# Projection chunks issued in halves instead of quarters on TensorE, in a decoder step with forgetting attention and gated linear attention

## The chip, the cores and the metric

The kernel runs on one core of a Trainium2 chip. The metric is the device time of one execution in microseconds (us); lower is better. A change of about 0.5% is the least that a measurement of this kernel can tell from none.

## The reference, cut to what matters

One layer of a decoder for a prompt of 1024 tokens and for 8 sequences with 8 new tokens each (64 columns more). Both are normalised and multiplied by one weight matrix, and two branches use the parts of the result:

```python
h = _rmsnorm(x, ln_g)
z = h @ w_in
fq, fk, fv, ff, fg, gq, gk, gv, glr, gg, ma, mb = jnp.split(z, SPLIT_POINTS, axis=-1)
...
o_f = _fox_prompt(fq, fk, fv, logf)      # softmax attention with a forget bias, 8 heads of 64
o_f = _fox_sample(..., cache_k, cache_v, cache_logf, page_table)   # 8 x 32 pages of 128 keys
o_g, s_end = _gla(gq, gk, gv, la, s0)    # 4 heads, state 128x256, chunks of 64 tokens
...
m = jax.nn.sigmoid(ma) * a + jax.nn.sigmoid(mb) * b
return x + m @ w_out
```

Everything is float32. The product `h @ w_in` is the largest piece of work: the kernel calls it the projection.

## The kernel before, in words

**Projection.** The weight matrix comes as tiles of 1024 x 128. For each tile n the 1088 token columns are done in three chunks c of 384, 384 and 320 columns. One chunk is 8 steps of contraction (KT_ = 8), and each step is three matmuls, since float32 is split into a high and a low part: `w_hi` with `h_hi`, `w_hi` with `h_lo`, `w_lo` with `h_hi` (L284, in `WeightStream.project`). So a chunk is 24 matmuls into one PSUM bank, and its last one raises the semaphore `w_projected`. Two banks take turns (`ring`), so the first matmul of a chunk waits on `z_read` until the chunk two before has been read out, and on `w_lo_set` for the tile's weights.

**Two stages that interleave.** The projection is independent work with which TensorE fills the time in which other work waits for ScalarE (ACT) or VectorE (DVE). The order is written out by planners ahead of time as one list of steps, and every engine walks the same list in its own order, waiting on semaphores only. A projection chunk stands in that list as four steps `("z", n, c, part)`, part 0 to 3, a quarter (6 matmuls) each. Between them the planners put the other steps, by estimated costs.

- `fox_order` (stage 1, forgetting attention of the prompt, `build_fox`): for head pair i and tile t of 128 queries: scores `sc` (L1061, TensorE), `sm` (L940 and L945, DVE: mask, bias, row extreme), `ex` (L803, ACT: exp), `pt` (L1071, TensorE: transposes of the probabilities into a bank of the lift ring, copied out by DVE at L566 for the first head and by ACT at L722 for the second), `pv` (L1084, L1089: weighting of the values), and `vt`, `kt`, `nm` (L1035, L1051).
- `schedule` (stage 2, `build_gla`): decode attention over pages (`kt`: four transposes of one page of keys, L1891, copied out by ACT at L1510 or DVE at L1391 in turn; `sc` L1906; `pt` L1922; `pv` L1939; `pn`, `pnv`, `od`) and gated linear attention (`att` L2005; `u` L2012, whose result DVE adds to the state at L1831; `o` L2019 and L2022; `og` L2030; `satt`, `so`, `sstate`; `decay`, `vturn`, `kturn`).

**The lift ring.** All transposes of pages and probabilities go through two PSUM banks that take turns: before the lifted step k, TensorE waits for the copy of step k-2. This wait is in `wait_bank`.

Stage 1 ends near 460 us of the trace, stage 2 near 1330 us. Behind them, four tiles of gates and `build_merge` project whole chunks; they don't use the part numbers.

ACT and DVE handlers stand on some `z` steps too (the split of the next weight tile into `w_hi` and `w_lo`, L254 and L259, at part 1 of a chunk), and SP issues the load of the next tile at part 1 of chunk 1.

Of the kernel before, what the change touches and what calls it, by code (L numbers as in the profile page):

```python
# [30 lines left out]
KT_ = D // P  # L31
# [259 lines left out]
FOX_PARTS = 4  # L291
# [145 lines left out]
def build_fox(nc, ins, outs, scratch, gates, sem, sb, psum, bank, con, vec, cc, vv, epsb, gq8, stream, os_fm, q_s, k_s, newb, glr):  # L437


    with ExitStack() as ctx:  # L440
# [128 lines left out]
        with nc.Block() as block:  # L569
# [422 lines left out]
            def _(pe):  # L992
# [32 lines left out]
                def z(n, c, part):  # L1025
                    if n < 2 and part == 0:
                        pe.wait_ge(h_lo_set, 2 * (3 * c + 3))
                    stream.project(pe, n, c, range(part * KT_ // FOX_PARTS, (part + 1) * KT_ // FOX_PARTS))

                def turn(st, src, p):  # L1030
                    wait_bank(pe, *st)
# [60 lines left out]
                def page_suffix(g):  # L1092
# [5 lines left out]
                              start=True, stop=True).then_inc(lifted, 1)  # L1098

                run(pe, {"xt": turn_x, "ff": forget, "lt": turn_logf, "z": z, "vt": v_turn, "kt": k_turn, "nm": norm_sum, "sc": scores, "pt": turn_prob, "pv": weigh, "lf": page_suffix})  # L1100


PARTS = 4
# [147 lines left out]
def build_gla(block, ins, outs, scratch, gates, sem, sb, psum, bank, cc, vv, epsb, stream, os_fm, q_s, k_s, newb, glr):  # L1251
# [7 lines left out]
    with ExitStack() as ctx:  # L1259
# [89 lines left out]
        for st in steps:  # L1349
            if st[0] in LIFTED:  # L1350
                n = len(lift_of)
# [530 lines left out]
        def _(pe):  # L1882
# [110 lines left out]
                turn(i, kdec, p, "kd_turned", "kd_set", p)  # L1993

            def z(n, c, part):
                stream.project(pe, n, c, range(part * KT_ // PARTS, (part + 1) * KT_ // PARTS))

            def att_step(i, t):
                if t == 0:
# [54 lines left out]
            def sstate(i, r):  # L2054
# [5 lines left out]
                for j in range(2):  # L2060
# [3 lines left out]

            run(pe, {"kt": kstep, "sc": sstep, "new": new, "pt": pstep, "pv": vstep, "pn": pn, "pnv": pnv, "od": od, "decay": decay,
                     "vturn": vturn, "kturn": kturn, "z": z, "att": att_step, "u": u_step, "o": o_step, "og": og,
                     "satt": satt, "so": so, "sstate": sstate, "sog": lambda i: og(i, TT)})

# [390 lines left out]
```

## Time and profile before

| What | us |
|---|---|
| median of 3 runs | 1675.98 (1675.61 to 1684.03) |
| the profiled execution | 1682.01 |
| its span, first to last instruction | 1680.2 |
| TensorE busy | 1548.9 (92%) |
| DVE busy | 671.7 (40%) |
| ACT busy | 614.6 (37%) |

TensorE has modelled ends for its matmuls, which overlap, so the distance from one start to the next says more than the busy share. Idle time of an engine is given with what released it. The granted clock of TensorE has a mean of 0.976 of full speed over the span; it has two levels, 1.0 (2.4 GHz) and 0.5 (1.2 GHz).

### The profile page before, as it was taken

The page shows a single profiled execution, that of the slowest core. Times are in us where ns is not written, and L with a number is a line of the kernel's source. Part 1 is how long each engine was busy: PE and PEld are TensorE (multiplying, and loading weights), DVE is VectorE, ACT ScalarE, POOL GpSimd, SP SyncE. Part 2 cuts the span into 40 slices and gives each one's busy share as a digit, 9 for nine tenths or more (in the row PEclk, how much of TensorE's full clock was granted, in tenths as well). Part 3 has the DMA queues.
Part 4 walks back from the last instruction along what each step waited for, and adds up shares of the span by engine and source line. Part 5 has one row for each costly group of instructions (what it writes and reads, how often), then busy time and mean ns, then how long its engine had stood idle before and what let it go on. Part 6 is the DMA issues. An engine that isn't in the chain of part 4 may idle for free.

```text
span 1680.2 us, 34414 instructions
## 1 busy us (share of the span) xinstructions
PE 1548.9 (92%) x11497; PEld 1290.4 (77%) x11497; DVE 671.7 (40%) x1504; ACT 614.6 (37%) x1311; POOL 501.6 (30%) x952
## 2 busy tenths in 40 slices
PE   6989998998799998999999999999998868999997
PEld 5878787776687876787877877778766767888987
DVE  4444343635344444534446344553443122233111
ACT  5344434444433434334444334433433243111111
POOL 3444344420090233432453332542330122111000
PEclk9999999998999999999999999999999889999999
DMA  4121212120165576776767676777656463322243
GB/s 166 31 82 43 67 43 81 56 77 28 53 207 172 166 228 181 240 229 185 242 215 253 213 216 202 223 235 227 191 170 204 132 216 101 118 97 71 79 117 93
DMA packets 156831, 250.00 MB, mean 149 GB/s; under 512 B 37449, under 2 KB 65610, under 8 KB 156146
## 3 DMA queue, kind: packets, MB, share of 16 engines
q1 hardware_dynamic: 125074, 215.78, 41.0%
q0 software_dynamic: 31584, 32.02, 6.3%
q8 instruction: 95, 1.56, 0.4%
q14 instruction: 78, 0.64, 0.1%
HBM read 217.47 MB, written 30.22 MB: 147 GB/s over the span
## 4 chain that ended last, share of the span: by engine, by line
PE 59%; ACT 3%; DVE 3%; DMA 3%; issue 2%; SPq 1%; POOL 0%; DVEq 0%; ACTq 0%
PE psum L284 29%; PE psum L1891 7%; PE psum L2341 6%; PE psum L1906 4%; PE psum L2333 4%; PE psum L1939 3%; DMA tmp_gates<-con 2%; PE psum L2012 1%; PE psum L2022 1%; DMA v_page<-in_cache_v 1%; PE psum L2019 1%; PE psum L1982 1%; PE psum L1922 1%; DVE w_lo L259 1%; PE psum L2030 1%
## 5 line engine op out<-in xcount | busy, mean ns | idle before, releaser
L284 PE MATMUL psum<-h_hi,w_hi 128*128 128x384 f32 (+1 forms) x1536 | 561.4, 365 | 38.1 <-DVEq L2278 15.0
L284 PE MATMUL psum<-h_hi,w_lo 128*128 128x384 f32 (+1 forms) x1536 | 511.6, 333 | 0.0
L284 PE MATMUL psum<-h_lo,w_hi 128*128 128x384 f32 (+1 forms) x1536 | 510.5, 332 | 0.0
L284 PEld LDWEIGHTS psum<-h_hi,w_hi 128*128 128x128 f32 x1536 | 295.7, 193 | 121.0 <-issue 107.0
L1461 POOL DMA_DIRECT2D sc<-tmp_bias x512 | 252.6, 502 | 308.9 <-PE psum L1922 306.0
L284 PEld LDWEIGHTS psum<-h_lo,w_hi 128*128 128x128 f32 x1536 | 296.6, 193 | 2.6 <-issue 0.3
L284 PEld LDWEIGHTS psum<-h_hi,w_lo 128*128 128x128 f32 x1536 | 295.0, 192 | 0.0
L670 POOL DMA_DIRECT2D lfp<-in_cache_logf x256 | 124.1, 485 | 178.1 <-issue 178.1
L1891 PE MATMUL psum<-con,k_page 128*128 128x128 f32 x1024 | 152.5, 276 | 9.6 <-DVE k_t L1391 6.3
L1510 ACT ACTIVATE k_t<-psum 128x512 f32<-128x512 f32 x128 | 76.1, 595 | 186.9 <-PE psum L1891 186.9
L1891 PEld LDWEIGHTS psum<-con,k_page 128*128 128x128 f32 x1024 | 120.9, 141 | 30.3 <-issue 26.2
L1391 DVE COPY k_t<-psum 128x512 f32<-128x512 f32 x128 | 88.2, 689 | 115.9 <-PE psum L1891 113.3
L259 DVE TENSOR_TENSOR w_lo<-w_raw,w_hi 128x1024 fp32r<-128x1024 f32 x70 | 85.6, 1223 | 92.8 <-ACT w_hi L254 92.2
L1939 PE MATMUL psum<-v_page,p_t 128*32 128x128 f32 x2048 | 72.4, 278 | 7.8 <-DMA v_page<-in_cache_v 7.7
L254 ACT ACTIVATE w_hi<-w_raw 128x1024 fp32r<-128x1024 f32 x70 | 73.3, 1047 | 8.7 <-PE psum L284 8.7
L2341 PE MATMUL psum<-o_hi,w_hi 128*128 128x384 f32 (+1 forms) x192 | 69.6, 362 | 0.0
L1939 PEld LDWEIGHTS psum<-v_page,p_t 128*32 128x32 f32 x2048 | 51.9, 110 | 22.6 <-issue 11.4
L1906 PE MATMUL psum<-k_t,q_bd 128*32 128x512 f32 x512 | 68.2, 605 | 0.0
L2333 PE MATMUL psum<-fox_o,up_a 128*128 128x384 f32 (+1 forms) x192 | 65.1, 484 | 3.3 <-issue 3.3
L2341 PE MATMUL psum<-o_lo,w_hi 128*128 128x384 f32 (+1 forms) x192 | 62.7, 327 | 0.0
L2341 PE MATMUL psum<-o_hi,w_lo 128*128 128x384 f32 (+1 forms) x192 | 62.6, 326 | 0.0
L2253 ACT ACTIVATE h_hi<-g_pair 128x384 fp32r<-128x384 f32 (+1 forms) x24 | 12.1, 505 | 129.8 <-DVE g_pair L2291 129.8
(237 smaller groups left out, 1950.4 us busy)
## 6 DMA issues: line engine op xcount, KB each, us to landing
k_page<-in_cache_k SPq DMA_DIRECT2D x256, 256.0 KB, 3.5
v_page<-in_cache_v SPq DMA_DIRECT2D x256, 256.0 KB, 3.1
w_raw<-in_w_tiles SPq DMA_DIRECT2D x63, 512.0 KB, 4.6
g_pair<-tmp_gates SPq DMA_DIRECT2D x16, 544.0 KB, 4.6
sc<-tmp_bias POOLq DMA_DIRECT2D x512, 16.0 KB, 2.9
tmp_ogla<-gate POOLq DMA_DIRECT2D x4, 1088.0 KB, 5.9
g_pair<-tmp_ogla SPq DMA_DIRECT2D x8, 544.0 KB, 5.3
x_in<-in_x_prompt SPq DMA_DIRECT2D x8, 512.0 KB, 6.5
```

The source lines that it names most:

```text
L254: act.activation(self.hi[:, k % 2], self.raw[:], ACT.Copy).then_inc(self.hi_set, 1)
L259: dve.tensor_tensor(self.lo[:, k % 2], self.raw[:], self.hi[:, k % 2].bitcast(F32), ALU.subtract).then_inc(self.lo_set, 1)
L284: m = pe.matmul(out, wt[:, s, k, :], h[:, k, t0:t0 + w], start=(k == 0 and a == 0), stop=(k == KT_ - 1 and a == 2))
L670: pool.dma_start(lfp[a % P:a % P + 1, a // P, :], ins["cache_logf"][ds(page, 1)] .rearrange("o p h -> o (p h)")).then_inc(lf_in[a // P], 16)
L1391: copy(k_t[:, p // 4 % 2, :, p % 4 * PAGE:(p % 4 + 1) * PAGE], quarters(lift_bank("kt", s, p))).then_inc(sig, 1)
L1461: pool.dma_start(sc[r0:r0 + TS, j % SLOTS, :], src.to_broadcast([TS, 512])).then_inc(sc_in[j % SLOTS], 16)
L1510: return A(out, in_, ACT.Copy)
L1891: m = pe.transpose(lift_bank("kt", s, p)[:, hp * P:(hp + 1) * P], k_page[a % NK][:, hp * P:(hp + 1) * P], cc("ident"))
L1906: m = MM(bank[5][32 * hp:32 * hp + 32, :], q_bd[:, hp, 16 * (1 - half):16 * (1 - half) + 32], k_t[:, n % 2, hp, :], start=(half == 0), sto ...
L1939: m = MM(bank[6][32 * hp:32 * hp + 32, 0:P], p_t[:, g % 2, col + 32 * hp:col + 32 * hp + 32], v_page[a % NV][:, hp * P:(hp + 1) * P], star ...
L2333: m = pe.matmul(bank[2 + c][:, 0:w], up_a[:, j % 2, k, :], fox_o[:, k, t0:t0 + w], start=(k == 0), stop=(k == NA - 1))
L2341: m = pe.matmul(bank[5 + c][:, 0:w], wt[:, s, k, :], v[:, k, t0:t0 + w], start=(k == 0 and a == 0), stop=(k == NBR - 1 and a == 2))
```

## The change

TensorE's handler of the step `z` in both stages issues two quarters at part 0 and two at part 2, and nothing at parts 1 and 3. The list of steps is the same, and the other engines' handlers are the same.

```diff
@@ build_fox, TensorE @@
                 def z(n, c, part):
                     if n < 2 and part == 0:
                         pe.wait_ge(h_lo_set, 2 * (3 * c + 3))
-                    stream.project(pe, n, c, range(part * KT_ // FOX_PARTS, (part + 1) * KT_ // FOX_PARTS))
+                    if part % 2 == 0:
+                        stream.project(pe, n, c, range(part * KT_ // FOX_PARTS, (part + 2) * KT_ // FOX_PARTS))
@@ build_gla, TensorE @@
             def z(n, c, part):
-                stream.project(pe, n, c, range(part * KT_ // PARTS, (part + 1) * KT_ // PARTS))
+                if part % 2 == 0:
+                    stream.project(pe, n, c, range(part * KT_ // PARTS, (part + 2) * KT_ // PARTS))
```

Two places of TensorE's order show what moves. (In the changed kernel line numbers are one or two higher.) The first is the start of head pair 1 in stage 1, behind the scores of tiles 0 and 1; L1071 are the transposes of the probabilities of tile 0, one for each head, and L1061 the scores of tile 2. Before:

```order
L1071 MATMUL psum<-con,prob 128x128
L284 MATMUL psum<-h_hi,w_hi 128x384
L284 MATMUL psum<-h_lo,w_hi 128x384
L284 MATMUL psum<-h_hi,w_lo 128x384
L284 MATMUL psum<-h_hi,w_hi 128x384
L284 MATMUL psum<-h_lo,w_hi 128x384
L284 MATMUL psum<-h_hi,w_lo 128x384
L1071 MATMUL psum<-con,prob 128x128
L1061 MATMUL psum<-k_fm,q_fm 128x384 x2
```

One quarter of the projection stands ahead of the first of these rows, right behind the scores of tile 1. Now twelve matmuls stand there, of which these are the last three:

```order
L284 MATMUL psum<-h_hi,w_hi 128x384
L284 MATMUL psum<-h_lo,w_hi 128x384
L284 MATMUL psum<-h_hi,w_lo 128x384
L1072 MATMUL psum<-con,prob 128x128 x2
L1062 MATMUL psum<-k_fm,q_fm 128x384 x2
```

The first transpose comes one quarter later, and nothing stands between the two.

The second is in stage 2, head 1, tile 3 of the linear attention: L2012 is `u`, L1891 the transposes of pages of keys, L2019 and L2022 are `o`, L1906 are decode scores. Before:

```order
L2012 MATMUL psum<-gv_tok,gk_tok 128x256 x2
L1891 MATMUL psum<-con,k_page 128x128 x8
L284 MATMUL psum<-h_hi,w_hi 128x384
L284 MATMUL psum<-h_lo,w_hi 128x384
L284 MATMUL psum<-h_hi,w_lo 128x384
L284 MATMUL psum<-h_hi,w_hi 128x384
L284 MATMUL psum<-h_lo,w_hi 128x384
L284 MATMUL psum<-h_hi,w_lo 128x384
L1891 MATMUL psum<-con,k_page 128x128 x4
L2019 MATMUL psum<-gv_tok,att 128x256
L2022 MATMUL psum<-state,q_in 64x256 x2
```

Now:

```order
L284 MATMUL psum<-h_hi,w_lo 128x384
L2014 MATMUL psum<-gv_tok,gk_tok 128x256 x2
L1892 MATMUL psum<-con,k_page 128x128 x12
L2021 MATMUL psum<-gv_tok,att 128x256
L2024 MATMUL psum<-state,q_in 64x256 x2
L1907 MATMUL psum<-k_t,q_bd 32x512 x4
```

The quarter between the second and the third page has moved ahead of `u`: three pages stand in a row, and no projection is left between `u` and `o`.

## Rows read from the trace of the kernel before

**Rows 1.** The page: span, and busy time of TensorE with its share.
```profile
span 1680.2 us, 34414 instructions
PE 1548.9 (92%) x11497; PEld 1290.4 (77%) x11497; DVE 671.7 (40%) x1504; ACT 614.6 (37%) x1311; POOL 501.6 (30%) x952
```

**Rows 2.** Windows by stage: busy us of each engine, PE clock, DMA share, GB/s.
```profile
90.00:465.00 375.00, 336.46 (x2371) 282.98 (x2370) 165.76 (x439) 159.27 (x341) 115.89 (x239) 0.96 0.20 58
465.00:560.00 95.00, 91.75 (x613) 78.10 (x612) 40.80 (x76) 34.41 (x67) 39.16 (x80) 0.97 0.61 184
560.00:1240.00 680.00, 659.65 (x5736) 526.08 (x5736) 312.21 (x716) 273.56 (x621) 258.98 (x517) 1.00 0.69 216
1240.00:1330.00 90.00, 74.24 (x689) 54.99 (x690) 30.56 (x87) 30.69 (x77) 12.80 (x24) 0.92 0.58 181
```

**Rows 3.** TensorE's waits, 90 to 465 us: total us, times, longest.
```profile
PE psum L1061 <- DVE nmin L945: 13.4, 11, 1.9
PE psum L1071 <- issue: 4.2, 10, 1.6
...
PE psum L1084 <- DVE prob_t L566: 2.8, 5, 0.8
```

**Rows 4.** TensorE's waits, 465 to 1330 us.
```profile
PE psum L2030 <- DVE o_n L1837: 12.0, 9, 4.9
...
PE psum L1891 <- DVE k_t L1391: 6.3, 6, 2.5
...
PE psum L1891 <- ACT k_t L1510: 2.7, 2, 2.4
```

**Rows 5.** Timeline, TensorE: start us, length us, instruction, count.
```profile
301.03 0.45 PE L284 MATMUL psum<-h_hi,w_hi 128*128 128x384 f32 x1
301.31 0.34 PE L284 MATMUL psum<-h_lo,w_hi 128*128 128x384 f32 x1
301.49 0.33 PE L284 MATMUL psum<-h_hi,w_lo 128*128 128x384 f32 x1
...
309.86 0.60 PE L1071 MATMUL psum<-con,prob 128*128 128x128 f32 x4
310.21 0.42 PE L284 MATMUL psum<-h_hi,w_hi 128*128 128x384 f32 x1
310.47 0.34 PE L284 MATMUL psum<-h_lo,w_hi 128*128 128x384 f32 x1
```

**Rows 6.** Timeline, two pages of keys, their copies, and the next page.
```profile
524.91 1.03 PE L1891 MATMUL psum<-con,k_page 128*128 128x128 f32 x8
525.54 0.60 ACT L1510 ACTIVATE k_t<-psum 128x512 f32<-128x512 f32 x1 [3.45 <-PE psum L1891]
525.98 0.69 DVE L1391 COPY k_t<-psum 128x512 f32<-128x512 f32 x1 [1.19 <-PE psum L1891]
```

**Rows 7.** Timeline, `u`, the state on DVE, and `o`.
```profile
1031.70 0.70 PE L2012 MATMUL psum<-gv_tok,gk_tok 64*128 64x256 f32 x4
1032.45 0.99 DVE L1831 SCALAR_TENSOR_TENSOR state<-state,e_last,psum 128x256 f32<-128x256 f32 x2 [2.52 <-PE psum L2012]
1033.60 0.67 PE L2019 MATMUL psum<-gv_tok,att 128*128 128x256 f32 x2 [1.19 <-DVE state L1831]
```

**Rows 8.** Timeline, start of head pair 1.
```profile
194.14 0.41 PE L1071 MATMUL psum<-con,prob 128*128 128x128 f32 x1
194.21 0.67 PE L284 MATMUL psum<-h_hi,w_hi 128*128 128x384 f32 x1
194.59 0.29 DVE L566 COPY prob_t<-psum 128x128 f32<-128x128 f32 x1 [3.84 <-PE psum L1071]
...
196.27 0.41 PE L1071 MATMUL psum<-con,prob 128*128 128x128 f32 x1
...
197.15 0.92 PE L1061 MATMUL psum<-k_fm,q_fm 64*128 64x384 f32 x4 [0.46 <-DVE nmin L945]
```

**Rows 9.** Window at the same place: columns as in rows 2.
```profile
190.00:197.00 7.00, 5.79 (x18) 4.56 (x18) 2.57 (x15) 3.21 (x10) 2.91 (x6) 0.52 0.13 47
```

## The prediction

> **What bounds the kernel now.** The page comes first: TensorE is busy for 1548.9 of 1680.2 us [rows 1]. The windows by stage then tell where the other time lies. Only stages 1 and 2 hold split chunks; in the windows from 90 to 1330 us TensorE is idle for 375 - 336.5 = 38.5, 3.2, 20.3 and 15.8 us [rows 2]. So TensorE sets the time, and a change can act in three ways: its own work gets cheaper, it waits longer or shorter, or its clock changes. The list of waits names the idle time. In stage 1 TensorE waits 13.4 us before scores for DVE's row extreme, and some 7 us around the transposes of probabilities [rows 3]. In stage 2 it waits 12.0 us for the normalised `o_n`, and 6.3 + 2.7 us, in 8 waits only, before the transposes of pages [rows 4]: 256 pages pass the two banks of the lift ring nearly without a stop, because of what stands between them. The timelines give the latencies that this work has to cover [rows 5 to 8].
>
> **What the change does.** No instruction is added or removed, and neither DVE, ACT, POOL nor SP gets another order. On TensorE each chunk's second quarter moves ahead of the steps that stood between parts 0 and 1, and its fourth ahead of those between 2 and 3. Every step in these two gaps is issued one quarter later than before, against the projection; steps in the other gaps keep their place. Counted in the printed orders and lists, the runs of projection work in stage 1 fall from 133 to 92, in stage 2 from 348 to 200. A quarter is 6 matmuls at 0.17 us from start to start, 1.0 us (0.9 for 320 columns). The loads of weights keep their conditions: `w_projected` of a chunk now comes up to a quarter earlier, which can only help them.
>
> **Term 1, fewer switches: -4 us.** Behind a step that uses part of the array (L1089, 128*64) the first matmul of a run takes 0.28 us until the next starts, against 0.17 to 0.18 later on: 0.10 us lost [rows 5]. Behind transposes it is otherwise: four of them and the first matmul take 310.47 - 309.86 = 0.61 us, which is 4 x 0.109 + 0.17, so nothing is lost [rows 5]. Of the 189 runs that go, 44 stood behind such a part-array step (120 to 83 in stage 2, 50 to 43 in stage 1). 44 x 0.10 = 4.4; some of it is paid by the transposes that follow instead, so -4. The bounds are 0 and, if each of the 189 cost 0.10, -19. The Trainium skill (TensorE: Matmul & The Clock Gate, step-by-step, LDWEIGHTS) says that the queue pulls the next weight load ahead while a matmul runs. By that rule a switch costs nothing and this term is 0; the 0.28 us say that here it is not all hidden, and I go by the row.
>
> **Term 2, the lift ring in stage 2: +13 us.** A page's transposes start at 524.91; the last of the four starts at 525.24, and ACT copies from 525.54 to 526.14 [rows 6]. The bank is then free for the page after the next, so between the end of one page (525.35) and the start of the next but one, 0.8 to 0.9 us of TensorE work must stand, 0.1 us more where DVE copies (0.69 us). I take 0.95. I added up the work between a page and the second lifted step behind it in both orders (page 0.44 us, quarter 1.0 or 0.9, other steps by their rows). Before, the least is 0.87 and the next 1.31: a shortfall of 0.1 us in all. Now 17 pairs have one page alone between them (0.44), and 24 have 0.65 to 0.91: 17 x 0.51 + 24 x 0.12 = 11.6 us. The probabilities of new tokens and the turned output use the same ring, 5 short pairs: 1.6 us. The sum is +13. It is a floor for each copy that starts at once; DVE and ACT are in order, and the 9.0 us of waits that the trace has with almost no shortfall are copies that stood behind something else [rows 4]. Against that, a wait covers its neighbour. Bounds: +5 and +30.
>
> **Term 3, linear attention: +4 us.** From the start of `u` to that of `o` are 1.90 us, of which `u` itself takes 0.64 and DVE's two state updates 0.99 [rows 7]; 1.26 us of other work would hide the wait, which was 1.19 us at this place. Pairs `u` to `o` with less: 5 before (2.5 us short in all), 11 now (6.8). `att` to `u`, which needs 0.85: 1.9 to 3.7; state steps of the samples, 1.6 more. These sum to 7.7, yet the steps between are often the pages of term 2, whose waits cover these, as in the second place of the order (three pages between `u` and `o`). So half, +4; bounds 0 and +9. The 12.0 us before `og` [rows 4] hardly change: the sum of what is missing there is 4.0 before and 3.7 now.
>
> **Term 4, the lift ring in stage 1: +8 us.** The same count, with 1.0 us as the need, has 14.3 us missing before and 35.5 now, as four lifted steps often stand in a row (two heads, two halves). Before, 14.3 on paper were some 7 us of waits in the trace [rows 3]. In a row of four every second wait is covered by the one before it. So the rise of 21 gives 21 x 0.5 = 10, less a little since ring copies wait behind scores on DVE that now have more time: +8. Bounds +3 and +18.
>
> **Term 5, starts of head pairs: +6 us.** TensorE transposes head 0's probabilities at 194.14, DVE copies them at 194.59 and only then takes the row extremes of tile 1, for which the scores of tile 2 wait until 197.15, 0.46 us idle [rows 8]. The first transpose now stands behind two quarters. At the clock of that moment a quarter is 2.1 us (194.21 to 196.27) [rows 8], so DVE's work and the scores of tile 2 come 2.1 us later, while TensorE has nothing more to do before them. The row extremes are what is late next, and the scores pay it all. Three of the four head pairs start so: 3 x 2.1 = +6. The fourth keeps its distances. At full clock it would be 3 x 1.0; bounds +2 and +8.
>
> **Term 6, the clock: +2 us.** From 190 to 197 us, behind the waits at such a start, the granted clock is 0.52, that is the lower level for nearly all of it [rows 9]. More idle time at the same places lets it stay there somewhat longer; one more such stretch of 3.5 us costs half of itself. Bounds -3 and +12.
>
> The sum is -4 + 13 + 4 + 8 + 6 + 2 = +29 us. Against the profiled execution of 1682.0 us this is 1711. That execution was 6.0 us over the median of 1676.0, so for the median I forecast **1705 us**, slower by 1.7%. 0.5% of the median is 8.4 us, which is what a measurement can tell from no change.
>
> **Rivals.**
> *The queues in order make it worse.* A late copy on DVE holds everything behind it: evacuations, then `z_read`, then the next chunk. For it speak the 9.0 us in 8 waits before pages [rows 4], 1.1 us each, far above a bare copy. If half of the 41 short pairs paid 1.1 us instead of 0.3, +16, and with the upper bounds of terms 4 and 6 another 20, the time is 1705 + 36 = 1741. Chance 0.19.
>
> *Backlog hides it.* If a page's copy overlaps what is still in the array better than the starts tell, terms 2 to 4 fall to a fifth, and head starts to 3: -4 + 5 + 3 = +4, 1680. Against it: waits at exactly such pairs are in the rows now [rows 3, 7]. Chance 0.09.
>
> *Freed queues, faster.* ACT and DVE stand at the head of their queues until a chunk's `w_projected`, and page copies and `o_n` stand behind. This signal now comes a quarter earlier. The price is in the 12.0 + 9.0 us of [rows 4]: if a wait for the chunk's end is most of it and shrinks by 1.0 us in each of these 17 waits, -17, and with -4 and ring waits of +5 the time is 1660. It decides from the point where more than half of stage 2's waits begin with a queue that stood on a chunk. Chance 0.05.
>
> *The clock recovers, faster.* Longer unbroken matmul work keeps the clock at 2.4 GHz, and the idle places don't grow. Windows at 0.96, 0.97, 1.00 and 0.92 [rows 2] leave 375 x 0.04 + 95 x 0.03 + 90 x 0.08 = 25 us below full speed. If 15 came back and terms 2 to 5 gave only 8, it is 1676 - 4 - 15 + 8 = 1665. Against it: the lower level begins behind waits at head starts, where no run gets longer ahead of them. The Trainium skill (TensorE: Matmul & The Clock Gate, HAM oscillation) advises to run all contraction steps of a tile together so that the array stays warm; it is this rule. Chance 0.04.
>
> **Numbers.** Forecast (1684 to 1725) 0.63, heavier 0.19, hidden 0.09, the two faster ones 0.09. The range reaches from 1682, above the hidden case's centre, to 1738, into the heavier one. Faster by over 0.5% has 0.09; within 0.5%, 1667.6 to 1684.4, takes most of the hidden case, 0.09; slower has 0.82.
>
> **What would show it.** TensorE's waits before L1891 (now L1892) rise from 9 to over 20 us, in some 40 waits, released by the copies of `k_t`; those before the next scores at head starts 0 to 2 rise from 0.46 to about 2.5 us; waits at L1084 rise; the first-of-run matmuls get fewer and the mean of `h_hi,w_hi` falls. The windows of stages 1 and 2 grow by about 15 us each, and nothing changes behind 1330 us but its start. The prediction is wrong if TensorE's idle time up to 1330 us grows by less than 10 us, or if the granted clock moves the time by more than its waits do.

## The result, and the profile after

| Kernel | median us | runs | ratio to before |
|---|---|---|---|
| before, same chip | 1680.01 | 4 (1675.61 to 1684.33) | |
| changed | 1735.53 | 4 (1732.52 to 1736.92) | 1.0332, 95% interval 1.0298 to 1.0366 |

The change costs 55.5 us, where the forecast had 29. The direction was right and so were most of the mechanisms. Their sizes were not, that of the clock above all, and one wait was left out. The profiled execution took 1736.92 us. Its page, first lines of what answers to [rows 1] and to the costliest groups:

```profile
span 1735.2 us, 34414 instructions
...
PE 1564.7 (90%) x11497; PEld 1303.0 (75%) x11497; DVE 669.0 (39%) x1504; ACT 609.1 (35%) x1311; POOL 501.7 (29%) x952
...
L284 PE MATMUL psum<-h_hi,w_hi 128*128 128x384 f32 (+1 forms) x1536 | 547.0, 356 | 42.6 <-DVEq L2280 14.9
...
L1892 PE MATMUL psum<-con,k_page 128*128 128x128 f32 x1024 | 150.7, 279 | 18.0 <-DVE k_t L1392 9.0
```

TensorE's busy time grew by 15.8 us and the time in which it was idle by 39.2 (1680.2 - 1548.9 = 131.3 before, 170.5 now). DVE and ACT do the same work as before. The pages alone now wait 18.0 us, and the line of the same group before is the second below:

```profile
L284 PE MATMUL psum<-h_hi,w_hi 128*128 128x384 f32 (+1 forms) x1536 | 561.4, 365 | 38.1 <-DVEq L2278 15.0
...
L1891 PE MATMUL psum<-con,k_page 128*128 128x128 f32 x1024 | 152.5, 276 | 9.6 <-DVE k_t L1391 6.3
```

For the stages, fixed windows no longer hold the same work. I cut both traces where the same chunk of the projection ends: the 10th, the 57th and the 156th update of `w_projected`. Columns as in [rows 2]. Before, and then after:

```profile
91.40:476.90 385.50, 346.94 (x2412) 292.61 (x2410) 169.99 (x449) 163.51 (x350) 127.11 (x262) 0.96 0.21 63
476.90:1315.00 838.10, 804.55 (x6925) 641.21 (x6926) 376.62 (x863) 330.27 (x746) 295.36 (x591) 0.99 0.68 210
1315.00:1680.20 365.20, 326.12 (x1765) 293.43 (x1763) 87.60 (x140) 77.88 (x133) 40.47 (x44) 0.96 0.34 111
```

```profile
89.30:503.30 414.00, 355.43 (x2411) 298.83 (x2412) 168.37 (x447) 161.18 (x348) 126.48 (x260) 0.94 0.20 59
503.30:1369.10 865.80, 811.36 (x6893) 647.70 (x6895) 374.83 (x863) 327.46 (x746) 296.60 (x593) 0.99 0.66 203
1369.10:1735.20 366.10, 327.75 (x1802) 294.44 (x1801) 88.27 (x142) 77.91 (x133) 40.62 (x44) 0.96 0.35 112
```

| Stage | longer by | TensorE idle | TensorE busy | (1 - clock) x duration |
|---|---|---|---|---|
| 1 | 28.5 | 38.6 to 58.6 | +8.5 | 17.1 to 23.9 |
| 2 | 27.7 | 33.6 to 54.4 | +6.8 | 5.1 to 11.9 |
| behind both | 0.9 | 39.1 to 38.4 | +1.6 | 14.7 to 15.4 |

The last column is worked out from the clock before it is rounded. It is the most that the lower level can have cost, as part of that time is idle anyway. Each stage gains about 20 us of waiting and up to 7 us of clock; nothing happens behind them. Over the whole span the clock's mean fell from 0.976 to 0.969.

One caution on single traces: in the traces of e8, e9 and e10 below, whose stage 2 has the code of before, stage 2 takes 842.7, 844.5 and 842.1 us, and in the trace of before 838.1. So every growth of stage 2 that is read against this one trace may be 4 to 6 us too large, that of the change too.

TensorE's waits in stage 1 (89 to 503 us), to be held against [rows 3]:

```profile
PE psum L1062 <- DVE nmin L945: 19.2, 10, 2.5
...
PE psum L1072 <- issue: 9.8, 20, 2.3
PE psum L1062 <- DVE q_fm L905: 7.7, 4, 1.9
PE psum L1085 <- ACT prob_t L722: 3.4, 6, 0.8
PE psum L1085 <- DVE prob_t L566: 3.3, 7, 0.5
```

The third row was not among those that I had rested anything on. Before, it read:

```profile
PE psum L1061 <- DVE q_fm L905: 3.5, 4, 0.9
```

In stage 2 (503 to 1369 us), against [rows 4]:

```profile
PE psum L2032 <- DVE o_n L1838: 15.2, 9, 4.7
PE psum L1892 <- DVE k_t L1392: 9.0, 10, 2.7
PE psum L1892 <- ACT k_t L1511: 6.4, 12, 2.4
PE psum L2021 <- DVE state L1832: 4.9, 11, 1.2
PE psum L2014 <- DVE att L1815: 4.6, 6, 1.4
...
PE psum L284 <- DVE k_in L1770: 1.9, 2, 1.3
PE psum L1892 <- ACT pn_t L1511: 1.5, 1, 1.5
```

Page waits went from 8 to 22 (9.0 to 15.4 us), `o` behind the state from 2 to 11 (1.8 to 4.9 us), and `og` behind `o_n` costs 3.2 us more.

The start of head pair 1, as in [rows 8], timeline of TensorE (in brackets, idle time before the instruction and what ended it):

```profile
197.53 0.49 PE L1062 MATMUL psum<-k_fm,q_fm 64*128 64x128 f32 x4 [1.93 <-DVE q_fm L905]
199.74 1.23 PE L1062 MATMUL psum<-k_fm,q_fm 64*128 64x256 f32 x4 [1.73 <-DVE nmin L945]
200.90 0.69 PE L284 MATMUL psum<-h_hi,w_hi 128*128 128x384 f32 x1
...
204.91 0.63 PE L1072 MATMUL psum<-con,prob 128*128 128x128 f32 x2
207.91 0.92 PE L1062 MATMUL psum<-k_fm,q_fm 64*128 64x384 f32 x4 [2.38 <-DVE nmin L945]
```

Three waits stand here. The scores of tile 1 wait 1.73 us, and did so before. The scores of tile 2 wait 2.38 us, about as term 5 had it (0.46 + 2.1 = 2.56). But the scores of tile 0 wait 1.93 us for `q_fm`, where it was 0.89. And the twelve matmuls from 200.90 on take 4.01 us, 0.32 from start to start after the first, so at the lower clock level.

A short pair of the lift ring in stage 2: three pages in a row. First TensorE, then ACT's copies, each from the timeline:

```profile
556.94 1.03 PE L1892 MATMUL psum<-con,k_page 128*128 128x128 f32 x8
558.32 0.63 PE L1892 MATMUL psum<-con,k_page 128*128 128x128 f32 x4 [0.34 <-ACT k_t L1511]
```

```profile
557.58 0.60 ACT L1511 ACTIVATE k_t<-psum 128x512 f32<-128x512 f32 x1 [3.78 <-PE psum L1892]
558.98 0.60 ACT L1511 ACTIVATE k_t<-psum 128x512 f32<-128x512 f32 x1 [0.81 <-PE psum L1892]
```

Eight transposes need 8 x 0.109 = 0.87 us from start to start, so the next page could have started at 557.81 and started at 558.32: 0.51 us lost, the figure of term 2. The list shows 0.34, because a wait is counted from the modelled end of the last transpose, 0.17 us behind the time when the next could start. Idle time under-counts each such wait by that much.

A worse one stands at 853 us, behind `u` (all engines):

```profile
852.47 0.70 PE L2014 MATMUL psum<-gv_tok,gk_tok 64*128 64x256 f32 x4
...
853.10 1.09 PE L1892 MATMUL psum<-con,k_page 128*128 128x128 f32 x8
853.27 1.00 DVE L1832 SCALAR_TENSOR_TENSOR state<-state,e_last,psum 128x256 f32<-128x256 f32 x2 [3.11 <-PE psum L2014]
854.19 0.68 DVE L1392 COPY k_t<-psum 128x512 f32<-128x512 f32 x1
...
855.02 0.63 PE L1892 MATMUL psum<-con,k_page 128*128 128x128 f32 x4 [0.82 <-DVE k_t L1392]
```

The copy of the first page starts only when DVE has updated the state, and the third page waits 0.82 us. This is the heavier rival's mechanism, one copy behind another piece of work on an engine that goes in order.

### The profile page after: what moved, and what is told of

Same layout as the page of the kernel before. It is cut to its first block, busy times and chain, and to the rows that moved or that the text cites. A ratio compares the mean times of both kernels' runs of the same rounds, so it can differ in the third digit from the quotient of the medians.

```text
span 1735.2 us, 34414 instructions
## 1 busy us (share of the span) xinstructions
PE 1564.7 (90%) x11497; PEld 1303.0 (75%) x11497; DVE 669.0 (39%) x1504; ACT 609.1 (35%) x1311; POOL 501.7 (29%) x952
## 4 chain that ended last, share of the span: by engine, by line
PE 57%; ACT 4%; DVE 4%; issue 3%; DMA 3%; SPq 1%; POOL 0%; DVEq 0%; ACTq 0%
PE psum L284 28%; PE psum L1892 6%; PE psum L2343 5%; PE psum L2335 3%; PE psum L1907 3%; PE psum L1940 3%; DMA tmp_gates<-con 2%; PE psum L2014 1%; PE psum L2024 1%; PE psum L2021 1%; DMA v_page<-in_cache_v 1%; PE psum L1983 1%; PE psum L1923 1%; DVE w_lo L259 1%; PE psum L2032 1%
## 5 line engine op out<-in xcount | busy, mean ns | idle before, releaser
L284 PE MATMUL psum<-h_hi,w_hi 128*128 128x384 f32 (+1 forms) x1536 | 547.0, 356 | 42.6 <-DVEq L2280 14.9
L1892 PE MATMUL psum<-con,k_page 128*128 128x128 f32 x1024 | 150.7, 279 | 18.0 <-DVE k_t L1392 9.0
L1892 PEld LDWEIGHTS psum<-con,k_page 128*128 128x128 f32 x1024 | 118.1, 142 | 44.4 <-issue 41.2
L1062 PE MATMUL psum<-k_fm,q_fm 64*128 64x512 f32 (+3 forms) x192 | 42.3, 544 | 27.0 <-DVE nmin L945 19.2
L566 DVE COPY prob_t<-psum 128x512 f32<-128x512 f32 (+3 forms) x48 | 26.7, 557 | 99.6 <-PE psum L1072 99.4
```

The costliest lines, as they stand in the source:

```text
L284: m = pe.matmul(out, wt[:, s, k, :], h[:, k, t0:t0 + w], start=(k == 0 and a == 0), stop=(k == KT_ - 1 and a == 2))
L1892: m = pe.transpose(lift_bank("kt", s, p)[:, hp * P:(hp + 1) * P], k_page[a % NK][:, hp * P:(hp + 1) * P], cc("ident"))
```

## The experiments

"Stage" figures are growth in the trace between the same chunks as above, against the trace of before. Small differences rest on more executions (up to 12 of a variant and 29 of before), so some ratios nearer to 1 than 0.5% still have an interval that leaves 1 out.

### Which stage: e1 and e2

e1 has halves in `build_fox` alone, e2 in `build_gla` alone (each is one of the two hunks of the change).

> Halves in stage 1 alone. The trace of the changed kernel has its 55 us in two equal parts: 28 by the end of stage 1, 28 in stage 2. Theory (each stage pays its own waits and its own lower clock): +26 to +30 us over before. Rival (a late stage 1 disturbs stage 2, for instance through the clock or the queues): under +20, or over +35. My prediction's terms for this stage gave +15.

> Halves in stage 2 alone. Theory: +26 to +30 us, the two stages add up to the whole. Rival: what is missing from the sum of both is coupling. My prediction's terms gave +14.

Measured: e1 1706.22 us, ratio 1.0160 (1.0122 to 1.0197), +27; e2 1706.05 us, 1.0154 (1.0132 to 1.0176), +26. They add up to 53 of the 55 us, and the intervals leave no room for more than a few us of coupling between the stages. Each costs about twice what I had given it.

### Stage 1 in two: e5 and e6

e5 joins quarters only in chunks 0 and 1 of the tile ahead of each head pair; e6 has the same condition with `not`.

```diff
+                    if n % 4 == 3 and n < 16 and c < 2:
+                        if part % 2 == 0:
+                            stream.project(pe, n, c, range(part * KT_ // FOX_PARTS, (part + 2) * KT_ // FOX_PARTS))
+                    else:
+                        stream.project(pe, n, c, range(part * KT_ // FOX_PARTS, (part + 1) * KT_ // FOX_PARTS))
```

> Halves only in the first two chunks of the gate tile of each head pair (chunks 0 and 1 of tiles 3, 7, 11, 15), 16 of stage 1's 108 pairs of quarters; quarters everywhere else. At head pair 1 the trace of the changed kernel has the norm of the last query chunk one quarter late (wait before the scores of tile 0 from 0.89 to 1.93 us), the transposes two quarters behind the scores of tile 1 (wait before the scores of tile 2 from 0.46 to 2.38) and 3.4 us more at the lower clock. Theory: 4.7 us for each of three heads and 1 for the fourth, +13 to +17 us. Rival (my term 5, transposes alone): +6. Rival (a share for every joined pair, 16/108 of 27): +4.

> Halves in the other 92 places of stage 1, quarters at the head starts. Theory: what is left of +27, so +10 to +14 us, from the lift ring and from the row extremes inside a head. Rival (a share for each): +23.

Measured: e5 1695.20 us, 1.0091 (1.0056 to 1.0125), +15; e6 1696.19 us, 1.0080 (1.0057 to 1.0103), +13. Eight of stage 1's 54 chunks carry half of its cost. The two halves are made differently. TensorE's idle time in the whole trace of e6 is 141.8 us, 10.5 more than before, and (1 - clock) x span, with the means over all executions, hardly moves (39.5 us for 38.5). In e5 stage 1 is idle for 46.6 us, 8.0 more than before, and the clock's share is 47.2 us for 38.5. What the clock costs in stage 1 comes from the starts of the head pairs.

### The start of a head pair in two: e9 and e10

The condition of e5 with `c == 0` (e9) and with `c == 1` (e10). The last norm of the queries, L1051, stands between the first two quarters of chunk 0; the transposes of tile 0 stand behind the first quarter of chunk 1.

> Quarters everywhere but in chunk 0 of the last tile ahead of each head pair (4 chunks in all), which goes in halves. All it does is to put the last norm of the queries one quarter later, so q_fm comes later for the scores of tile 0. Theory (the prediction left this out, and it is about half of what the starts of head pairs cost): the wait before the first scores rises from 0.9 to about 1.9 us in four places, and a stretch at the lower clock begins earlier, together +5 to +9 us over before (1685 to 1689). Rival (the norm is covered, all of the cost of the starts comes from the late transposes): 0 to +2 us.

> Quarters everywhere but in chunk 1 of the last tile ahead of each head pair (4 chunks), which goes in halves: the transposes of the probabilities of tile 0 come one quarter later, the norm keeps its place. This is term 5 of the prediction alone: +6 us over before, and with one more stretch at the lower clock at each start +6 to +9 (1686 to 1689). Rival (the late norm is harmless and this is everything): +13 to +17 (1693 to 1697).

Measured: e9 1687.62 us, 1.0038 (1.0017 to 1.0058), +6.4; e10 1689.16 us, 1.0047 (1.0027 to 1.0066), +7.9. Together 14, nearly all of e5. TensorE's waits in stage 1 of e9, then of e10, against 13.4 and 3.5 before:

```profile
PE psum L1065 <- DVE nmin L945: 11.7, 10, 1.9
...
PE psum L1065 <- DVE q_fm L905: 7.7, 4, 1.9
```

```profile
PE psum L1065 <- DVE nmin L945: 17.4, 10, 2.5
...
PE psum L1065 <- DVE q_fm L905: 3.6, 4, 0.9
```

Each edit raises its own wait. e10 leaves that for `q_fm`, and e9 lowers that for `nmin` by 1.7 us. The late norm is a cause of its own, which the prediction did not have.

But the waits are only about half of either cost. TensorE's idle time in stage 1 is 38.6 us before, 41.3 in e9 and 42.7 in e10, so 2.7 and 4.2 us more. The mean granted clock over 12 executions is 0.975 in both, against 0.978 in 29 executions of before; times the span this is 42.7 and 42.9 us, for 37.3. The other 5 us or so are clock.

### Stage 2 in two: e3 and e4

The 204 joins of stage 2 were sorted by the counts of terms 2 and 3, with 1.05 us as the need of the ring. e3 makes the 42 that leave a pair of the ring short. e4 makes 145 that take nothing from a pair, of ring or linear attention, that needs it. The other 17 leave a pair of linear attention short and none of the ring; they are in neither. `LISTED` holds the 42 in e3; in e4 it holds the 59 that are not joined, and the test is `not in`.

```diff
...
+                half = part // 2
+                if n * 6 + c * 2 + half in LISTED:
+                    if part % 2 == 0:
+                        stream.project(pe, n, c, range(half * KT_ // 2, (half + 1) * KT_ // 2))
+                else:
+                    stream.project(pe, n, c, range(part * KT_ // PARTS, (part + 1) * KT_ // PARTS))
```

> Stage 2 with quarters, but for 42 of its 204 pairs of quarters: those whose joining leaves less than 1.05 us of work between a lifted step and the next but one (all 18.7 us of the ring's shortfall on paper come from them). Theory (the two banks of the ring are what costs, and DVE's and ACT's queues behind them): +16 to +22 us. Rival (every joined pair costs its share, since steps come late and fill is coarse): 42/204 of 29 = +6 us.

> Stage 2 with halves in 145 of 204 places, and quarters in the 59 where joining makes a pair of the lift ring or a pair of linear attention (u to o, att to u, og to u) short. Theory (only short pairs cost): -3 to +3 us, with fewer runs of projection work than before. Rival (a share for every joined pair): 145/204 of 29 = +21 us.

Measured: e3 1690.54 us, 1.0050 (1.0031 to 1.0068), +8, in the trace of stage 2 +13.1 (the trace is that of its fastest execution, 1683.96 us); e4 1689.04 us, 1.0049 (1.0032 to 1.0065), +8, in stage 2 +11.5. By the caution above the stage figures are 4 to 6 us too large, and then they agree with the times. Both theories were too simple. The 42 joins cost 0.2 us each; the others, which by the count should have cost nothing, 0.06 each, as much in sum. Page waits in the two (costliest groups, e3 and then e4):

```profile
L1892 PE MATMUL psum<-con,k_page 128*128 128x128 f32 x1024 | 152.1, 277 | 16.9 <-DVE k_t L1392 8.6
```

```profile
L1892 PE MATMUL psum<-con,k_page 128*128 128x128 f32 x1024 | 151.6, 278 | 12.1 <-DVE k_t L1392 7.1
```

e3 has nearly all of the change's 18.0 us, e4 only 2.5 more than before. So term 2's count did find the pages that wait. Stage 2 of e4 is idle for 8.8 us more, spread over `o_n` (13.9 for 12.0), pages, chunks that wait for DVE (1.9 and 0.7) and others. No single one of them was isolated, and why 145 joins with enough on paper cost 8 us stays open.

### Late or long: e11

Both stages in halves, but at the place of the second quarter:

```diff
+                    if part % 2 == 1:
+                        stream.project(pe, n, c, range((part - 1) * KT_ // FOX_PARTS, (part + 1) * KT_ // FOX_PARTS))
```

> Both stages in halves, but a half is issued where its second quarter stood, at parts 1 and 3. The same gaps are emptied as in the change, so two pages or four transposes stand in a row as often, but the steps in them come a quarter earlier against the projection instead of a quarter later. Theory (the length of the pieces costs, by what is left between dependent steps): stage 2 grows by 20 to 30 us as in the change, and stage 1 by 10 to 20 (the starts of head pairs are partly spared, since norm and transposes come earlier), together 1708 to 1732. Rival (what costs is that steps come late, not the length of the pieces): each stage grows by under 8 us, 1680 to 1695.

Measured: 1708.61 us, ratio 1.0162 (1.0132 to 1.0193), +27. Stages 1 and 2 of its trace:

```profile
92.90:480.50 387.60, 343.64 (x2413) 290.48 (x2414) 171.16 (x450) 164.20 (x351) 126.25 (x259) 0.97 0.21 61
480.50:1345.30 864.80, 811.26 (x6927) 650.30 (x6929) 375.40 (x861) 328.40 (x743) 298.11 (x593) 0.98 0.65 204
```

The expectation has a mistake: these halves do not empty the same gaps, but the other ones, between parts 3 and 0 and between 1 and 2. The count has to be made again. By it, stage 2 is 12.7 us short in the ring, about the 13 of the change; stage 1 is 27 us short, against 14 before and 36 in the change. Stage 2 indeed grows by 26.7 us, as in the change (27.7), though the steps that move are early here instead of late, and its idle time grows by 20.0 us (20.8 in the change). There the size of the pieces costs, not that they push work back. Stage 1 grows by 2.1 us only, where the change has 28.5. The norm is no longer late: no wait for `q_fm` is left in the list of waits, and the clock's share of the stage falls from 17.1 to 11.9. All idle time of the stage grows by 5.4 us. The largest new wait is not one of the ring: norms of queries and keys, which now come early, wait 3.2 us for their squares (L1052, behind ACT L760), and the scores wait 15.9 us for `nmin` (13.4 before). So the ring's part is below 5 us for the 13 that are missing more, and in this stage the count with the rule of term 4 (half, 6.5) is neither confirmed nor clearly wrong. "Long" rules stage 2 and "late" rules the starts of stage 1, and neither theory holds for both. Over the whole program e11 has the clock of before (0.978 in both, means of all executions; in its trace stage 1 has 5 us less of the clock's share and stage 2 has 8.5 more), so its 27 us are waits in the main.

### Smaller pieces: e7, e8, e12

e7 keeps quarters and moves one of them between the scores of tiles 0 and 1 at each start. (`fill` is the planner's list of projection steps.)

```diff
+            if s == ("sc", i, 1):
+                for _ in range(2):
+                    placed += fill[0][1]
+                    steps.append(fill.pop(0)[0])
```

e8 plans stage 1 in eighths:

```diff
-            out.append((("z", n, c, part), 1.05))
+            out += [(("z", n, c, part), 0.525), (("zz", n, c, part), 0.525)]
...
-                    stream.project(pe, n, c, range(part * KT_ // FOX_PARTS, (part + 1) * KT_ // FOX_PARTS))
+                    stream.project(pe, n, c, range(2 * part, 2 * part + 1))
+
+                def zz(n, c, part):
+                    stream.project(pe, n, c, range(2 * part + 1, 2 * part + 2))
```

e12 does so in both stages, with four eighths moved as in e7.

> The kernel before with quarters; at each of the four head starts the first quarter behind the scores of tile 1 moves between the scores of tile 0 and of tile 1, into the 1.7 us that TensorE waits there for the row extremes. If fill at the right place is what counts and the clock falls because of this idle time: -4 us from waits (1.0 each, the transposes come early too) and up to -14 from the clock, -6 to -18 in all. Rival: the quarter is then missing before the scores of tile 2, which wait the same time later, and the clock falls all the same: -2 to +4.

> Stage 1 with eighths: each quarter is two list items of three matmuls, which the planner places by half the cost each; steps that belong behind a quarter stand behind its second item. Theory (waits grow with the size of a piece of fill): the opposite of the halves at less than half the size, -4 to -12 us. Rival (switches cost more than the waits give back, or waits at this size are set by the chains alone): 0 to +8.

> Both stages in eighths (three matmuls each), planned as steps of their own at half the cost, and at the starts of head pairs four of them between the scores of tile 0 and tile 1. Stage 1 in eighths gave -8, the moved quarter -4 by itself (partly the same idle time). Theory (waits at dependent steps go with the size of the pieces): stage 1 -8 to -12, stage 2 -3 to -9, together 1659 to 1669. Rival (stage 2 has no cover to win, its waits are for DVE's work on o_n, and more switches behind part-array steps cost 0.1 us each): stage 2 0 to +6, together 1668 to 1678.

Measured: e7 1676.19 us, ratio 0.9977 (0.9960 to 0.9995); e8 1674.69 us, 0.9952 (0.9927 to 0.9978); e12 1674.48 us, 0.9968 (0.9948 to 0.9987).

e7 gains 4 us, less than its theory had. Its rival was right on the waits: at head pair 1 the scores of tile 1 wait 0.48 us for 1.73, but those of tile 2 wait 2.15 us for 0.46, and all waits for `nmin` are 12.6 us for 13.4. It was wrong on the clock, which rose (means of all executions 0.980 for 0.977, 5 us of time).

Stage 1 of e8 is 7.9 us shorter, with 5 us less idle time:

```profile
88.70:466.30 377.60, 344.23 (x2412) 288.92 (x2410) 169.74 (x449) 163.81 (x350) 128.24 (x264) 0.97 0.23 65
```

In e12 stage 1 gains no more than in e8 (377.6 us again), and stage 2 gains nothing (841.5 us against 838.1). The rival's time holds there. Of 33.6 us of idle time before, 12.0 are waits for `o_n` and 4.4 for loads of value pages, and with smaller pieces these are 10.7 and 4.7 us. TensorE is busy there for 4.5 us more at the same clock share (5.1 us). That fits the rival's dearer switches; it was not taken apart. e8 and e12 are both faster than the kernel before, by 0.5% and 0.3%, and their intervals overlap; e8, the smaller edit, is the best version found.

## Why the prediction was right or wrong

**Term 1, -4.** It was not measured by itself, and stays open. Fewer first-of-run matmuls show in the mean of `h_hi,w_hi` (365 to 356 ns), but these are modelled durations which overlap.

**Term 2, +13.** Right in kind, near in size. Waits before L1891, now L1892, went from 9.6 to 18.0 us, those for the copy of `pn` included (0.4 to 1.5); with 0.17 for each of some 15 new waits that makes 11. A bare wait costs the 0.51 us of the sum. "From 9 to over 20 us, in some 40 waits" was too much: 15.4 us in 22 waits.

**Term 3, +4.** Too small. The waits grew for `state` by 3.1 us, for `att` by 1.0, for `o_n` by 3.2; with smaller ones that is about 9, the upper bound. "The 12.0 us before `og` hardly change" failed: my count looked at the distance from `o` to `og` on TensorE alone. That what stands ahead of `o_n` on ACT and DVE is the reason is likely, and no run isolated it. Waits of chunks for DVE (`k_in`, `sig`), 2.4 us more, were in no term.

**Term 4, +8.** Too small: e6 measures 13, nearly all of it waits (idle time +10.5 us). `L1072 <- issue` rose from 4.2 to 9.8 us in the change and in e6 alike. The waits of scores for `nmin` rose too, from 13.4 to 16.4 in e6, and my count looked at the ring alone.

**Term 5, +6: a step that failed.** For the transposes the path was right: in e10 the scores of tile 2 wait 2.49 us at the first three starts, for 1.43, 0.46 and 0.46 before, and 1.92 at the fourth, as before. Their sum is 5.1 us, where I had 6, and some of it comes back at later waits (4.2 us more idle time in all). But "the fourth keeps its distances" looked at the transposes alone. At all four starts a second step, the last norm of the queries, moves one quarter back too, and nothing covers it: scores of tile 0 wait 1.93 us for 0.89 (e9, +6.4). I had counted the steps behind the start and not the one ahead of it. Both together cost 15 us (e5), of which 8.0 are idle time and most of the rest is clock.

**Term 6, +2: the second failure, and the larger one.** By the traces the clock accounts for up to 12.6 us of the 55 ((1 - clock) x span, before rounding, 40.3 and 52.9 us); by means over the executions it is 48.9 us in the changed kernel and 37.3 to 38.5 in that of before, 10 to 12 us. So it was worth five to six times the forecast and stands at my upper bound of 12. I had priced one more stretch of 3.5 us. The growth is about seven of them, in both stages, and the starts of head pairs alone bring 5 us with either of their two late steps (e9, e10).

The prediction gives two ranges, 1684 to 1725 and 1682 to 1738. The median, 1735.5, is outside the first and at the edge of the second, and the growth is nearly double the forecast one.

The forecast's condition for being wrong, that the clock moves more than the waits do, did not come true: idle time +39, clock at most +13.

**Rivals.** Hidden backlog and both faster cases fell. The faster clock by longer unbroken runs went the other way: 0.969 for 0.976 with halves, and 0.980 with eighths in stage 1 (e8), by the view of span and clock. The Trainium skill (TensorE: Matmul & The Clock Gate, HAM oscillation) blames waits between bursts for the loss of clock, and that half of it agrees with the trace (0.79 behind waits of 1.74, 1.74 and 3.97 us, shown in the last section); its remedy, to run the contraction steps of a tile together, lengthened the waits here (131.3 to 170.5 us idle). The heavier rival, 1741, came nearest to 1735.5. Its mechanism, a copy held up behind other work, is seen at 853 us, but as one contribution: e2 with all of stage 2 costs 26 us (22 to 30), where this case adds 16 to the 14 that my terms gave to that stage.

## What to carry to other kernels

When independent work fills the waits of a chain, the piece must be smaller than the slack between two dependent steps; count that slack for every step that moves, those ahead of the place as well as those behind it. Then add the clock: new waits of 1 to 2 us at the starts of head pairs brought stretches of several us at half speed with them. Here the idle time that can be counted was about three quarters of the bill, and at those starts about half. To find out whether long pieces or late steps cost, issue the same pieces at their end: here that gave one stage back and left the other.

## What the runs showed of the hardware

**What the clock costs.** In 29 executions of the kernel before, the time ran from 1672.0 to 1689.6 us and the granted clock from 0.982 to 0.972, and the two go together: 1.6 us of time for each 0.001 of clock (correlation -0.94). The whole span would give 1.7. So the spread between executions of the same code is mostly clock, and time at the lower level is paid nearly in full.

**Where it falls.** In the trace of before, 40.3 x 2 = 81 us lie at the lower level, and 52.9 x 2 = 106 us in the changed kernel. One new place is near the end of stage 2, where a head's sampled tokens are done; the windows begin at the same steps, before and after:

```profile
1265.00:1289.00 24.00, 19.75 (x202) 15.01 (x204) 10.41 (x34) 8.66 (x23) 1.62 (x3) 1.00 0.61 192
```

```profile
1318.00:1342.00 24.00, 16.32 (x155) 12.36 (x148) 7.69 (x29) 6.70 (x18) 0.54 (x1) 0.79 0.44 138
```

Before, TensorE waited here 2.72 us at the most and kept 1.00. Now waits of 1.74, 1.74 and 3.97 us stand within 16 us, the clock falls to 0.79, and 155 matmuls are done instead of 202. A stretch at half speed (0.32 us from start to start) follows the second of the waits, and another the third:

```profile
1320.69 0.43 PE L1940 MATMUL psum<-v_page,p_t 128*32 128x128 f32 x8 [1.74 <-DMA v_page<-in_cache_v]
...
1324.16 0.66 PE L2032 MATMUL psum<-con,o_n 128*128 128x128 f32 x2 [1.74 <-DVE o_n L1838]
...
1336.26 0.66 PE L2032 MATMUL psum<-con,o_n 128*128 128x128 f32 x2 [3.97 <-DVE o_n L1838]
```

In e3, which has nearly all of the change's page waits, (1 - clock) x duration of stage 2 is 4.1 us, for 5.1 before, and the mean clock of its six executions is 0.980, for 0.978: short waits that are spread out did not lower the clock there. The share also differs by some us between executions of the same code (behind both stages 14.7 us before and 9.2 in e3), so of a single trace only a difference as large as the change's says much.
